# Where a 20 MB zero fill is issued, and where its landing is waited for, in a two-block network kernel

## The reference, cut to what matters

```
mod_x = silu(c) @ w_ada + b_ada                        # and mod_c from c_ctx
p_x = modulate(rmsnorm(x, norm_mix_w), sh1, sc1) @ w_in     # q k v g r_f r_b pool_in
p_c = modulate(rmsnorm(ctx, norm_mix_w), csh1, csc1) @ w_in
gk  = log_sigmoid(r @ w_gk + b_gk) / 16
o   = gla_bidir(...)        # chunked scan, states from the context
mix = concat(gla_output(o, g), pool_project(pool_grid(pool_in)))
h   = x + g1 * (mix @ w_out)
h   = h + g2 * moe(modulate(rmsnorm(h), sh2, sc2), ...)
```

## Time and profile before

| | us |
|---|---|
| median of three runs | 2198.26 |
| profiled execution | 2182.58 |
| its span, first to last instruction | 2180.7 |
| TensorE busy | 2087.6 (96%) |
| VectorE busy | 974.0 (45%) |
| GpSimd busy | 218.2 (10%) |
| scan layer's first matmul | at 218.89 |
| output projection's first matmul | at 285.44 |
| zero fill, issue to landing | 103.3 |

### The profile page before, as it was taken

One profiled execution on the slowest core, in us unless ns is written; L12 is line 12 of the kernel. 1 busy time (PEld: TensorE's weight loads), 2 busy tenths in 40 slices (PEclk: granted clock), 3 DMA queues, 4 the chain that ended last, 5 costly groups with the idle time before them and its releaser, 6 DMA issues.

```text
span 2180.7 us, 36117 instructions
## 1 busy us (share of the span) xinstructions
PE 2087.6 (96%) x14969; PEld 1030.8 (47%) x14969; DVE 974.0 (45%) x1651; ACT 495.3 (23%) x878; POOL 218.2 (10%) x266
## 2 busy tenths in 40 slices
PE   5959899999999999999999999899999999999998
PEld 2824545333333333333333333688484448777643
DVE  2511535742232223223322345754577625597742
ACT  2400312111111011101110110311126102666560
POOL 1000001112211221122112222200000000000000
PEclk9979899999999999999999999999999999999999
DMA  9972325999999999999999999713121032212200
GB/s 376 337 293 91 146 109 229 415 412 424 418 415 420 423 418 420 423 420 423 418 421 417 421 421 418 286 69 109 39 105 50 1 105 78 97 58 97 97 20 39
DMA packets 111832, 565.90 MB, mean 259 GB/s; under 512 B 16933, under 2 KB 29010, under 8 KB 77938
## 3 DMA queue, kind: packets, MB, share of 16 engines
q1 hardware_dynamic: 88950, 512.93, 58.1%
q0 software_dynamic: 19584, 49.84, 6.4%
q10 hardware_dynamic: 3228, 2.17, 0.3%
HBM read 545.21 MB, written 37.62 MB: 267 GB/s over the span
## 4 chain that ended last, share of the span: by engine, by line
PE 79%; DVE 3%; DMA 3%; issue 1%; ACT 1%; ACTq 0%; POOL 0%; SPq 0%; POOLq 0%; DVEq 0%
PE ps L2425 30%; PE ps L461 11%; PE ps L2395 9%; PE ps L3964 5%; PE ps L2403 5%; PE ps L3863 4%; PE ps L449 3%; PE ps L1649 2%; PE ps L3843 2%; DMA ring<-in_w_gu 1%; PE ps L3395 1%; PE ps L3386 1%; DMA ring<-in_odd_w_in 1%; PE ps L3015 1%; PE ps L3059 1%
## 5 line engine op out<-in xcount | busy, mean ns | idle before, releaser
L2425 PE MATMUL ps<-ring,xeT 128*32 128x512 f32 x6144 | 668.1, 593 | 4.8 <-DMA ring<-in_w_gu 4.1
L2425 PEld LDWEIGHTS ps<-ring,xeT 128*32 128x32 f32 x6144 | 196.3, 110 | 447.2 <-issue 440.4
L2395 PE MATMUL ps<-ring,mT 128*32 128x512 f32 x2048 | 266.6, 592 | 0.0
L2164 DVE TENSOR_TENSOR mT<-ps,spread_bias 128x768 f32<-128x768 f32 x32 | 30.6, 957 | 433.8 <-PE ps L2425 433.8
L2102 ACT ACTIVATE mT<-mT 128x768 f32<-128x768 f32 x32 | 27.0, 843 | 851.0 <-DVE mT L2164 851.0
L461 PE MATMUL ps<-hT_late,ring 128*128 128x256 f32 x704 | 157.7, 383 | 0.4 <-issue 0.4
L2403 PE MATMUL ps<-ring,mT 128*32 128x256 f32 x2048 | 157.4, 379 | 0.0
L461 PEld LDWEIGHTS ps<-hT_late,ring 128*128 128x128 f32 x704 | 135.0, 192 | 22.4 <-issue 3.7
L2403 PEld LDWEIGHTS ps<-ring,mT 128*32 128x32 f32 x2048 | 66.6, 110 | 153.2 <-issue 153.2
L3964 PE MATMUL ps<-ring,mT 128*128 128x512 f32 x256 | 110.4, 592 | 0.0
L1924 POOL DMA_INDIRECT xe<-xn_scratch,idx x93 | 96.5, 1037 | 31.4 <-issue 29.7
(11 more groups left out here) (517 smaller groups left out, 2569.0 us busy)
## 6 DMA issues: line engine op xcount, KB each, us to landing
ring<-in_w_gu SPq DMA_DIRECT2D x128, 2048.0 KB, 11.1
ring<-in_w_down SPq DMA_DIRECT2D x128, 1024.0 KB, 11.5
y_scratch<-zeros POOLq DMA_DIRECT2D x1, 20352.0 KB, 103.3
ring<-in_even_w_in SPq DMA_DIRECT2D x18, 1024.0 KB, 9.3
ring<-in_w_ada SPq DMA_DIRECT2D x32, 512.0 KB, 11.7
ring<-in_odd_w_in SPq DMA_DIRECT2D x16, 1024.0 KB, 7.7
ring<-in_w_ada SPq DMA_DIRECT2D x8, 1024.0 KB, 17.6
ring<-in_w_in SPq DMA_DIRECT2D x8, 1024.0 KB, 20.7
```

Source lines behind the costliest of these rows:

```text
L2395: mm = nc.tensor.matmul(quad(b, 2 * q + n), acted(k, q, src), w[:, kk, n * BANK:(n + 1) * BANK], start=first, stop=last)
L2425: mm = nc.tensor.matmul(quad(q, c), left(q), part_columns(w, c), start=start, stop=stop)
```

## The change

The fill is no longer issued when the modulation vectors are ready (`mod_ready`), but when TensorE has finished the first product of the second panel (`p_vp.p1`). The wait for its landing moves from the end of GpSimd's list in the projection layer's block to the end of its list in the scan layer's block. The fill itself is unchanged.

```diff
                 scol_zeroed.on(nc.gpsimd.memset(zeros[:], 0.0))
                 scol_zeroed.wait(pool)
-                pool.wait_ge(mod_ready.sem, 3)
+                p_vp.p1.filled(pool)
                 rows_zeroed.on(pool.dma_start(
                     y_dram.rearrange("r (h n) -> (r h) n", n=BANK).rearrange("(p a) n -> p a n", p=CAP),
                     zeros[0:CAP, :].unsqueeze(1).to_broadcast([CAP, (E + XB) * D // BANK, BANK])), 16)
-                rows_zeroed.wait(pool)
@@ scan layer's block
                 for a in amat:
                     amat_zero.on(nc.gpsimd.memset(a, 0.0))
+                rows_zeroed.wait(pool)
```

## The result

The changed kernel takes 2226.47 us (median, 2222.52 to 2228.32), the kernel before 2198.66 beside it: ratio 1.0121, 95% interval 1.0092 to 1.0150. The forecast was 2195.4, with a range up to 2206 and a chance of 0.16 for slower. It was wrong, in the size and in the direction. Ratios and intervals are worked out over all runs, so they can differ a little from the quotient of two medians.

The account below looks back on a forecast made before the run. TensorE and loads issued relative to it were taken to bound the first 285 us. Terms -21.1 + 12.0 + 3.9 + 1.8 + 0.5 = -2.9 us took the median 2198.26 to 2195.4; range 2182 to 2206.

Parts of the forecast that it names:

- What bounds the kernel: First 285 us: TensorE and loads issued relative to it; the 13.25 us gap before the second panel waits for loads.
- The fill taken away from tiles 16 to 23: First vector cluster and second panel: without the fill the panel's first product starts at 125.5, not 146.63: 21.1 us gained.
- The stall given back in the second cluster: Second vector cluster, tiles 28 to 31: takes the first's 19.26 us, not 7.29, so 12.0 us lost.
- The scan layer's first loads: Behind tile 31: `w_pool` and first pooling matrix take 9.5 us, there at 216.1 against 212.2 wanted; clock costs 1.8 us.
- the third rival: Scan layer starves: row loads and matrices come later than 0.138 MB per us; at 240, +7 net, 2205; chance 0.12.
- The moved wait: End of scan block: fill lands between 225 and 250, block ends about 281, 30 us of cover; removing old wait gives nothing.
- the second rival: GpSimd held at projection block's end until its own queue is empty: scan starts at 232, +13, 2211; chance 0.07.
- The rival's price: If GpSimd is held at the projection block's end: fill lands at 231, scan starts at 232, not 218.89: +13, 2211.

Follow-up runs that it names:

- two halves of the change: Kernel before with only the wait moved to the scan layer's block: ratio 1.0005; with only the fill's place of issue moved: ratio 1.0134.
- the quarter fill: Kernel before plus a second fill of a quarter, issued by GpSimd behind product p4 and waited for in the scan layer's block: 2214.59 against 2196.74 us.
- the small clear: Changed kernel plus one small unread clear on GpSimd right behind the fill's issue, in the same block: 2207.15 against 2182.36 us.
- the first experiment: Kernel before with only the wait for the landing moved to the scan layer's block, fill still at 42 us: 2198.15 against 2196.74 us.

## Why the prediction was wrong, step by step

*What bounds the kernel* was read rightly: the 13.25 us gap was a wait for tiles under the fill, and it shrank to between 3.7 and 5.8 us when the fill left (the changed kernel and the experiments that move or split the fill).

*The fill taken away from tiles 16 to 23*: forecast 21.1 us, measured 18.85 (146.63 to 127.78). The cluster took 8.9 us, not 7.3, and the product 10.15, not 8.88, as its start was at the low clock for longer (0.50 from 127.78 to 133.5; before, from 146.63 to 150). So the second cluster started at 192.80, not 189.3. A term mis-sized by 3.5 us.

*The stall given back in the second cluster*: forecast 19.26 us for the whole cluster, measured 22.25 (192.80 to 215.05). The mechanism was right, and its price 3 us short. The fill that was left when tile 16 set out in the old place was 8.2 MB, not 7: by 94 us 12.6 MB had moved. The Trainium skill (DMA: Bandwidth & Descriptors, Arbitration) says that each DMA engine takes turns between its queues, a packet at a time. The estimate that the prediction made from it, a loss of 1 to 2 us (with the last tile 8.4 us after the start and its eight matmuls behind it, it is some 2), is not what this trace shows: the cluster lost 15.0.

*The scan layer's first loads* is the second step that failed: forecast 9.5 us behind tile 31 for the first matrix, measured 19.9 (213.1 to 233). In the changed kernel it was issued at 199.27, and landed 33.7 us later, at 233; the forecast had 216. The 0.138 MB per us, taken from tiles 20 and 21, was twice what came: 1.31 MB in 19.9 us are 0.066. Nobody waited for it, since the meeting was held until 246. On this queue the first pooling product would thus have started some 12 us later than before even without the hold (233 against 221.29), by my estimate from the landing; it wasn't run. That is the third rival, the starved scan. On ScalarE's queue, with the same bytes in three parts, the first matrix was there at 212.

*The moved wait* is the step that failed first, and the one that the measured time comes from: the scan layer started at 246.93, 30.6 us behind where the second cluster's end would have let it start (216.3). It is not alone in the sign, since by the estimate above the late matrix would have made the kernel slower without it too. The prediction said that nothing is queued behind the wait but the meeting of the scan block, and that the fill had 30 us of cover there. In fact the fill had no cover at all: it had to be down by the end of the projection layer's block, at about 216. The two halves of the change show it (1.0005 and 1.0134), the quarter fill shows it with another size, the small clear shows that it is the block's end, and ScalarE's fill that it is GpSimd's (or that of its kind of queue). I had this as the second rival, at 0.07, because SyncE passes such an end with loads under way. SyncE's q1 and GpSimd's q0 are different kinds of queue in the profile ("hardware_dynamic" and "software_dynamic"), and I took the one for evidence on the other. No row of before shows GpSimd pass an end with a DMA under way; with both outcomes open, 0.07 was far too low for a mechanism that undoes the whole edit.

*The rival's price* was short as well: 231 for the landing and 13 us, against 246.33 and 27 to 28. I divided what was left by 0.28 to 0.30 MB per us for all engines together. Near the end the engines together moved 0.05 MB per us, a sixth of that, with a share of 0.17: a few engines still had their part to finish. The tail had been there to see: 0.15 MB in 140:145. The Trainium skill, DMA: Bandwidth & Descriptors (its row on DMA engines 7 and 15), says that two of the sixteen are usually slower; the 50 GB/s in that stretch agree with a few engines left, and no view here names them.

## What to carry to other kernels

Before moving a wait out of a block, ask what the block's end waits for. Here GpSimd doesn't reach the meeting of a block while a DMA that it issued is under way, so its transfers must fit into the block, whether a wait for them is written there or not; ScalarE's and SyncE's may run on. A long transfer that nobody needs soon is best cut so that each part fits a stretch in which the DMA engines are idle; here two parts gave 0.7 to 0.8%, and neither place alone did. And a transfer ends with its last DMA engine: read the tail in the slices (here 50 GB/s for 15 us), not the mean rate.

## What the hardware showed that was not expected

- GpSimd held at the block's end until its own DMA is down: it goes on 0.41, 0.44 and 0.44 us after the landing in the changed kernel, with the small clear (20,352 KB both) and with the 4,992 KB, and 0.76 us after it (246.21 against 137.85 + 107.6) where the wait is also written in the block. No instruction of kernel.py in that block asks for this in the first three; whether the chip does it or the way in which the end of a block is built isn't shown.
- The same 20.84 MB leaves other loads more room from ScalarE's queue in three DMAs than from GpSimd's in one: the second cluster took 13.0 us and not 22.25. One difference stands in the queues, of the changed kernel in 180:200 and of ScalarE's fill in 130:260: GpSimd's packets hold 4.1 KB, ScalarE's 2.0.

```profile
q0 software_dynamic: 1022, 4.19, 65.3%
```
```profile
q10 hardware_dynamic: 10224, 20.84, 50.9%
```

Whether the packets, the kind of queue or the three parts do it stays open.
- Issuing isn't free on ScalarE: the third part held it 30.74 us. On GpSimd the whole fill took 3.23.
- The scan layer took 66.5 us before and 62.75 in the first experiment, with the same instructions. The stretches show a clock of 0.76 against 1.00 between 251 and 267:

```profile
251.00:267.00 16.00, 12.56 (x105) 7.65 (x104) 11.21 (x23) 4.60 (x8) 0.00 (x0) 0.76 0.00 1
```
```profile
251.00:267.00 16.00, 11.32 (x129) 7.46 (x127) 11.14 (x23) 5.83 (x11) 0.00 (x0) 1.00 0.00 1
```

The first is the kernel before, the second the first experiment. TensorE had idled within the stretch in both, 3.44 us up to 258.55 and 3.25 us up to 258.48; the clock fell behind that in the one and stayed at 1.00 in the other. So a few us of a single trace can be the clock's luck and not the edit's.
